# Feed-forward up projection with 512-column matmuls of high and low activations, and halves added on ScalarE and VectorE

## The chip, the cores and the metric

The kernel runs on one NeuronCore of a Trainium2 chip. The metric is the device time of one execution in microseconds, and of several executions the median counts. TensorE (PE) multiplies, VectorE (DVE), ScalarE (ACT) and GpSimd (POOL) do the elementwise work, SyncE (SP) issues most of the loads.

## What is computed

The program is a whole small model: two layers of a first block (feed-forward, mixer, feed-forward; the mixers are a short convolution and a sparse attention) and two layers of a second block. 256 tokens, model width 1024, everything in fp32. The change touches the feed-forward, which the first block calls four times:

```python
def rmsnorm(x, g):
    xf = x.astype(jnp.float32)
    y = xf * lax.rsqrt(jnp.mean(xf * xf, axis=-1, keepdims=True) + EPS)
    return (y * g.astype(jnp.float32)).astype(x.dtype)

def swiglu_ffn(x, w_in, w_out):          # w_in 1024 x 5632, w_out 2816 x 1024
    gate, up = jnp.split(x @ w_in, 2, axis=-1)
    return (jax.nn.silu(gate) * up) @ w_out

for i in range(DEPTH):                   # DEPTH = 2
    if i == N_A_LAYERS:
        kv = shared_kv(h, ...)
    h = h + 0.5 * swiglu_ffn(rmsnorm(h, ffn1_norm[i]), ffn1_w_in[i], ffn1_w_out[i])
    ...                                  # mixer
    h = h + 0.5 * swiglu_ffn(rmsnorm(h, ffn2_norm[i]), ffn2_w_in[i], ffn2_w_out[i])
```

## The kernel before

Activations lie transposed, features on the partitions and the 256 tokens along the row. fp32 products are made of three matmuls of a faster fp32 type (fp32r): a value is split into a high part (rounded to that type) and a low part (the rest), and `mm3` adds high x high, high weight x low activation, and low weight x high activation (lines 712, 713 and 714). The activations are `hnh` and `hnl`, eight tiles of 128 x 256 each; of the weights, `wah`/`wal` hold a chunk of the up projection and `wbh`/`wbl` one of the down projection, two buffers each.

A feed-forward stage walks over 22 chunks of 128 hidden features. `up` of a chunk (PE) makes gate and up, the two sides `g`, over `KT` = 8 k-steps: 2 x 8 x 3 = 48 matmuls into one PSUM bank, 256 columns for each side; banks 4 and 5 take turns. Its end is `gu_ready`. VectorE multiplies the bank by the tokens' factor `rln` into `tmp` (line 1781, `gs_ready`), ScalarE applies silu (line 1332), VectorE multiplies by the up side (1785) and splits the product into `hidh` and `hidl` (1716, 1717, `hid_ready`). `down` of the chunk (PE, `add_rows`) is 8 x 3 = 24 matmuls that add to all 1024 outputs in banks 0 to 3. `staged` sets PE's order: up 0, up 1, down 0, up 2, down 1, and so on to up 21, down 20, down 21. There is no scheduler: each engine runs its own program as it is written, and semaphores tie them together.

Around a chunk, ScalarE also makes the high parts of the weights (`hi_a`, line 1213, and `hi_b`, line 1220), VectorE the low part `wal` (`lo_a`, line 1663) and GpSimd `wbl` (`lo_b`, line 2287); SyncE loads the next raw weights once the low parts have been made. In chunk 0, PE starts each k-step as soon as its activations are there, between two matmuls with zeros that open and close the bank (`open_bank` 717, `close_bank` 720). After it, in stages with `sums`, PE sums the squares (697), ScalarE takes the root and loads the table of silu, and VectorE inverts the root (1653) before line 1781 can run. `open_acc` (725) opens banks 0 to 3. In the first stage VectorE has further `tasks` behind chunks 1, 3, 4, 6 and 7: it copies parameters, reduces angles and makes cosines (lines 1994 to 2013). "Stage" below is one of the four feed-forward stages; in the profile they are at some 16 to 203, 301 to 487, 535 to 727 and 861 to 1046 us.

Of the kernel before, what the change touches and what calls it, by code (L numbers as in the profile page):

```python
# [18 lines left out]
F32R = mybir.dt.float32r  # L19
# [6 lines left out]
P = 128  # L26
# [75 lines left out]
def build(nc, a, out):  # L102
    ctx = ExitStack()
    with ctx:
# [42 lines left out]
        silu, hf = gate_hid[:, 0:2], gate_hid[:, 2:4]  # L147
        hidh, hidl = sb("hidh", [P, 2, T], F32R), sb("hidl", [P, 2, T], F32R)
        hnh, hnl = sb("hnh", [P, KT, T], F32R), sb("hnl", [P, KT, T], F32R)
# [16 lines left out]
        bank = [psum[:, 512 * i:512 * (i + 1)] for i in range(8)]  # L166

# [492 lines left out]
        def _(pe):  # L660
# [85 lines left out]
            def ffn(sums=True, extra=lambda: None, halves=False):  # L746
                n["hn"] += 4

                def up(i, u):
# [4 lines left out]
                    s, at = (n["sa"] + u) % 2, 4 + (n["ffn"] + u) % 2  # L754
                    b = bank[at]
                    if i is FIRST and u == 0:
                        for k in range(KT):
# [3 lines left out]
                            if k == 0:  # L761
                                open_bank(at)
                            for g in range(2):
                                c = slice(g * P, (g + 1) * P)
                                mm3(b[:, g * T:(g + 1) * T], wah[:, s, k, c], wal[:, s, k, c],
                                    hnh[:, k, :], hnl[:, k, :], False, False)
                        close_bank(at).then_inc(S("gu_ready"), 1)
                        return
                    for g in range(2):
                        c = slice(g * P, (g + 1) * P)  # L770
                        for k in range(KT):
                            m = mm3(b[:, g * T:(g + 1) * T], wah[:, s, k, c], wal[:, s, k, c],
                                    hnh[:, k, :], hnl[:, k, :], k == 0, k == KT - 1)
# [7 lines left out]
                def after_first():  # L781
                    if sums:
                        sum_folded()
                    extra()
# [206 lines left out]
            def rest_of_parameters():  # L991
# [3 lines left out]
                pe.wait_ge(S("tcmp_copied"), 1)  # L995
                pe.transpose(bank[6][:, 0:120], vecs[0:120, 0, :], cst[0:120, C_ID:C_ID + 120])
                pe.transpose(bank[6][:, 128:160], vecs[0:32, 1, :], cst[0:32, C_ID:C_ID + 32]
# [13 lines left out]
            for v in range(2):  # L1011
                pe.wait_ge(S("blk_ready"), 8 * (v + 1))
                if v == 1:
                    pe.wait_ge(S("rt_ready"), n["rn"])
                for j in range(16):
                    x = mm(bank[7 - v][:, 0:60], w1s[v][:, j, :], blk[:, v, j, :], start=j == 0, stop=j == 15)
                x.then_inc(S("cmp_ready"), 1)

            ffn(sums=False)

            pe.wait_ge(S("hcmp_ready"), 2)
# [1371 lines left out]
```

## Time and profile before

| | us |
|---|---|
| median of 3 executions | 1385.82 |
| lowest, highest | 1383.04, 1401.29 |
| span of the profiled execution, first to last instruction | 1378.9 |
| PE busy in it | 1301.2 (94%) |
| PE weight loads busy | 1240.3 (90%) |
| DVE, ACT, POOL busy | 869.8, 618.5, 432.9 |

The profiled execution is one of its own; the profile gives its span and no time around it. Its span is 6.9 us below the median. PE stands for the matmuls and PEld for the weight loads that overlap them. Matmuls are pipelined, so a matmul's duration is longer than its pitch, the distance from one start to the next. An idle time in square brackets stands ahead of the instruction, with what ended it.

### The profile page before, as it was taken

What the parts mean: (1) busy time and instruction counts of PE and PEld (TensorE: products, weight loads), DVE (VectorE), ACT (ScalarE), POOL (GpSimd) and SP (SyncE); (2) the same over time, 40 slices, a digit from 0 to 9 for tenths busy, and PEclk for the clock granted to TensorE, in tenths of its full rate; (3) what the DMA queues carried; (4) which work ended last, traced back from release to release, by engine and by line L of the source; (5) the groups of instructions that cost most, each with busy time, mean ns of one, the idle gap of its engine ahead of it and who ended that gap; (6) DMA issues with size and microseconds to landing.
All of it is one profiled execution on the core that took longest, in us unless ns stands there. A gap on an engine that the chain in (4) does not pass through costs nothing.

```text
span 1378.9 us, 27323 instructions
## 1 busy us (share of the span) xinstructions
PE 1301.2 (94%) x10717; PEld 1240.3 (90%) x10717; DVE 869.8 (63%) x1373; ACT 618.5 (45%) x927; POOL 432.9 (31%) x200
## 2 busy tenths in 40 slices
PE   7999999999999998999999889999999998879878
PEld 6999998989999998999999658899999996778768
DVE  6685458786555466444446785755446686875586
ACT  5343344344443355333335685543334436434381
POOL 2444432214444424444440242344441002400041
PEclk8999999999999999999998899999999999999989
DMA  8778655656776546666643215566663453334310
GB/s 257 204 220 242 198 167 152 178 175 203 231 221 183 182 154 176 186 187 189 187 152 126 60 42 152 160 205 185 184 199 97 147 166 147 111 99 146 123 31 32
DMA packets 275115, 222.52 MB, mean 161 GB/s; under 512 B 8098, under 2 KB 256438, under 8 KB 274924
## 3 DMA queue, kind: packets, MB, share of 16 engines
q1 hardware_dynamic: 272528, 215.59, 51.5%
q0 software_dynamic: 1504, 4.49, 1.5%
q10 hardware_dynamic: 1020, 1.58, 0.3%
q8 instruction: 41, 0.67, 0.2%
q14 instruction: 22, 0.18, 0.0%
HBM read 216.40 MB, written 4.19 MB: 160 GB/s over the span
## 4 chain that ended last, share of the span: by engine, by line
PE 76%; DVE 12%; ACT 7%; issue 2%; DMA 1%; ACTq 0%; POOL 0%; DVEq 0%; SPq 0%; POOLq 0%
PE psum L712 24%; PE psum L713 24%; PE psum L714 23%; DVE wal L1663 2%; ACT pbuf L1459 2%; DVE wal L1846 1%; ACT hnh L1294 1%; ACT wah L1213 1%; DVE hnl L1681 1%; DVE hnh L1716 1%; ACT tmp L1459 1%; PE psum L675 1%; ACT arena L1298 1%; ACT wah L1250 1%; PE psum L1141 1%
## 5 line engine op out<-in xcount | busy, mean ns | idle before, releaser
L712 PE MATMUL psum<-hnh,wah 128*128 128x256 f32 (+1 forms) x2176 | 617.6, 284 | 15.0 <-DVE wal L1663 8.2
L713 PE MATMUL psum<-hnl,wah 128*128 128x256 f32 (+1 forms) x2176 | 609.1, 280 | 0.0
L714 PE MATMUL psum<-hnh,wal 128*128 128x256 f32 (+1 forms) x2176 | 608.8, 280 | 0.0
L2287 POOL TENSOR_TENSOR wbl<-raw_b,wbh 128x1024 fp32r<-128x1024 f32 x96 | 324.2, 3378 | 535.2 <-ACT wbh L1220 460.8
L712 PEld LDWEIGHTS psum<-hnh,wah 128*128 128x128 f32 (+1 forms) x2176 | 415.4, 191 | 22.7 <-issue 11.5
L713 PEld LDWEIGHTS psum<-hnl,wah 128*128 128x128 f32 (+1 forms) x2176 | 413.5, 190 | 2.3 <-issue 1.7
L714 PEld LDWEIGHTS psum<-hnh,wal 128*128 128x128 f32 (+1 forms) x2176 | 413.9, 190 | 0.0
L1663 DVE TENSOR_TENSOR wal<-raw_a,wah 128x2048 fp32r<-128x2048 f32 (+1 forms) x128 | 295.5, 2308 | 101.3 <-ACT wah L1213 100.2
L1213 ACT ACTIVATE wah<-raw_a 128x2048 fp32r<-128x2048 f32 (+1 forms) x126 | 237.3, 1884 | 94.0 <-PE psum L714 88.9
L1332 ACT ACTIVATE gate_hid<-tmp 128x256 f32<-128x256 f32 x88 | 36.7, 417 | 430.4 <-DVE tmp L1781 430.4
L712 PE MATMUL psum<-hidh,wbh 128*128 128x256 f32 x768 | 213.2, 278 | 0.9 <-DVE hidl L1717 0.9
L713 PE MATMUL psum<-hidl,wbh 128*128 128x256 f32 x768 | 213.0, 277 | 0.0
L714 PE MATMUL psum<-hidh,wbl 128*128 128x256 f32 x768 | 213.0, 277 | 0.0
L1781 DVE TENSOR_TENSOR tmp<-psum,rms 128x512 f32<-128x512 f32 x88 | 60.8, 691 | 224.1 <-PE psum L714 217.0
L712 PEld LDWEIGHTS psum<-hidh,wbh 128*128 128x128 f32 x768 | 145.0, 189 | 1.1 <-DVE hidl L1717 1.1
L714 PEld LDWEIGHTS psum<-hidh,wbl 128*128 128x128 f32 x768 | 144.2, 188 | 0.0
L713 PEld LDWEIGHTS psum<-hidl,wbh 128*128 128x128 f32 x768 | 144.1, 188 | 0.0
L2350 POOL TENSOR_SCALAR pbuf<-pbuf,rs 128x256 f32<-128x256 f32 x36 | 33.9, 951 | 334.9 <-DVE rs L1903 258.5
L1220 ACT ACTIVATE wbh<-raw_b 128x1024 fp32r<-128x1024 f32 x96 | 100.2, 1044 | 8.5 <-PE psum L714 4.3
L1785 DVE TENSOR_TENSOR gate_hid<-gate_hid,tmp 128x256 f32<-128x256 f32 x88 | 39.5, 449 | 43.3 <-ACT gate_hid L1332 43.3
L1459 ACT ACTIVATE pbuf<-pbuf,nmx 128x256 f32<-128x256 f32 (+1 forms) x108 | 44.0, 410 | 6.5 <-DVE nmx L1896 3.8
L1294 ACT ACTIVATE hnh<-hres,par 128x256 fp32r<-128x256 f32 x72 | 31.4, 499 | 30.4 <-DVE hres L1736 19.2
(298 smaller groups left out, 1510.3 us busy)
## 6 DMA issues: line engine op xcount, KB each, us to landing
raw_a<-in_ffn_w_in SPq DMA_DIRECT2D x176, 512.0 KB, 5.1
raw_b<-in_ffn_w_out SPq DMA_DIRECT2D x88, 512.0 KB, 5.0
raw_a<-in_w_in_even SPq DMA_DIRECT2D x15, 1024.0 KB, 5.3
raw_a<-in_conv_w_in SPq DMA_DIRECT2D x24, 512.0 KB, 4.1
raw_a<-in_w_in_odd SPq DMA_DIRECT2D x11, 1024.0 KB, 5.3
raw_a<-in_w_kv SPq DMA_DIRECT2D x6, 1024.0 KB, 5.5
raw_b<-in_conv_w_out SPq DMA_DIRECT2D x8, 512.0 KB, 5.7
raw_a<-in_attn_w_q SPq DMA_DIRECT2D x4, 1024.0 KB, 5.2
```

Source lines behind the costliest of these rows:

```text
L712: mm(dst, wh, xh, start=start, stop=False)
L713: mm(dst, wh, xl, start=False, stop=False)
L714: return mm(dst, wl, xh, start=False, stop=stop)
L1213: act.activation(wah[:, s, :, 0:w], raw_a[:, wa.slot(u), :, 0:w], ACT.Copy).then_inc(S("a_hi"), 1)
L1220: act.activation(wbh[:, s], raw_b[:, s], ACT.Copy).then_inc(S("b_hi"), 1)
L1294: x = act.activation(hnh[:, t, :], hres[:, t, :], ACT.Copy, scale=gains[:, g, t:t + 1])
L1332: act.activation(silu[:, gs, :], tmp[:, gs, 0:T], ACT.Silu).then_inc(S("silu_ready"), 1)
L1459: x = act.activation(p[:, lo:hi], p[:, lo:hi], ACT.Exp, scale=-1.0 if duos[st]["kind"] == "full" else 1.0, bias=nmx[:, r, i:i + 1], accum_ ...
L1663: v.tensor_tensor(wal[:, s, :, 0:w], raw_a[:, (n["ra"] + u) % 2, :, 0:w], wah[:, s, :, 0:w].bitcast(F32), ALU.subtract).then_inc(S("a_lo"), 1)
L1781: v.tensor_tensor(tmp[:, gs, :].rearrange("p (g c) -> p g c", g=2), bank[4 + gs][:, :].rearrange("p (g c) -> p g c", g=2), rln[:, None, :] ...
L1785: link(v.tensor_tensor(hf[:, hs, :], silu[:, gs, :], tmp[:, gs, T:2 * T], ALU.mult))
L2287: g.tensor_tensor(wbl[:, s], raw_b[:, s], wbh[:, s].bitcast(F32), ALU.subtract).then_inc(S("b_lo"), 1)
```

## The change

PE's two matmuls with the same high weights become one of 512 columns: high activations on the left, low ones on the right, into one whole bank per side. For that the activations are one tensor `hn2`. The matmul of the low weights and the high activations stays, 256 columns, on the left half. A chunk now takes two banks, 4 and 5 for even chunks and 6 and 5 for odd ones, so bank 5 is used by each chunk for the second side, and `up` waits in its middle for the addition of the chunk before. ScalarE copies both right halves into `halves_sb` (`low_copied`), VectorE adds them to the left halves into `tmp` (`gs_ready`) and then multiplies `tmp` by `rln` in place (`gu_scaled`), and silu comes after that. The zero matmuls of chunk 0 go. As bank 6 is now taken, the transposed parameters and the compression's products move to other banks, with the waits that go with them.

```diff
-        hnh, hnl = sb("hnh", [P, KT, T], F32R), sb("hnl", [P, KT, T], F32R)
+        hn2 = sb("hn2", [P, 2, KT, T], F32R)
+        hnh, hnl = hn2[:, 0], hn2[:, 1]
...
+        halves_sb = ptb[:, :, :].rearrange("p a c -> p (a c)")[:, 0:1024].rearrange("p (b g c) -> p b g c", b=2, g=2)
+
+        def up_banks(p):
+
+            return bank[4 + 2 * p], bank[5]
+
+        def up_halves(p, half):
+
+            both = psum[:, 512 * (4 + p):512 * (6 + p)].rearrange("p (b c) -> p b c", b=2)
+            return both[:, :, half * T:(half + 1) * T]
...
                     pe.wait_ge(S("gs_ready"), n["ffn"] + u + 1 + 2 * i)
-                    s, at = (n["sa"] + u) % 2, 4 + (n["ffn"] + u) % 2
-                    b = bank[at]
+                    s, pair = (n["sa"] + u) % 2, up_banks((n["ffn"] + u) % 2)
+
+                    def product(g, k):
+
+                        c = slice(g * P, (g + 1) * P)
+                        mm(pair[g][:, :], wah[:, s, k, c], hn2[:, :, k, :], start=k == 0, stop=False)
+                        return mm(pair[g][:, 0:T], wal[:, s, k, c], hnh[:, k, :], start=False, stop=k == KT - 1)
+
                     if i is FIRST and u == 0:
                         for k in range(KT):
                             if halves and k % 4 == 0:
                                 pe.wait_ge(S("first_lo"), k // 4 + 1)
                             wait_hn(k)
-                            if k == 0:
-                                open_bank(at)
                             for g in range(2):
-                                c = slice(g * P, (g + 1) * P)
-                                mm3(b[:, g * T:(g + 1) * T], wah[:, s, k, c], wal[:, s, k, c],
-                                    hnh[:, k, :], hnl[:, k, :], False, False)
-                        close_bank(at).then_inc(S("gu_ready"), 1)
+                                m = product(g, k)
+                        m.then_inc(S("gu_ready"), 1)
                         return
                     for g in range(2):
-                        c = slice(g * P, (g + 1) * P)
+                        if g == 1:
+                            pe.wait_ge(S("gs_ready"), n["ffn"] + u + 2 + 2 * i)
                         for k in range(KT):
-                            m = mm3(b[:, g * T:(g + 1) * T], wah[:, s, k, c], wal[:, s, k, c],
-                                    hnh[:, k, :], hnl[:, k, :], k == 0, k == KT - 1)
+                            m = product(g, k)
                     m.then_inc(S("gu_ready"), 1)
...
-                    act.wait_ge(S("gs_ready"), n["ffn"] + u + 3 + 2 * i)
-                    act.activation(silu[:, gs, :], tmp[:, gs, 0:T], ACT.Silu).then_inc(S("silu_ready"), 1)
+                    act.wait_ge(S("gu_ready"), n["ffn"] + u + 1 + 2 * i)
+                    act.activation(halves_sb[:, gs], up_halves(gs, 1), ACT.Copy).then_inc(S("low_copied"), 1)
+                    act.wait_ge(S("gu_scaled"), n["ffn"] + u + 1 + 2 * i)
+                    act.activation(silu[:, gs, :], raw_gate[gs], ACT.Silu).then_inc(S("silu_ready"), 1)
...
-                    v.wait_ge(S("gu_ready"), n["ffn"] + u + 1 + 2 * i)
-                    v.tensor_tensor(tmp[:, gs, :].rearrange("p (g c) -> p g c", g=2),
-                                    bank[4 + gs][:, :].rearrange("p (g c) -> p g c", g=2),
-                                    rln[:, None, :].to_broadcast([P, 2, T]), ALU.mult).then_inc(S("gs_ready"), 1)
+                    gu = tmp[:, gs, :].rearrange("p (g c) -> p g c", g=2)
+                    v.wait_ge(S("low_copied"), n["ffn"] + u + 1 + 2 * i)
+                    v.tensor_tensor(gu, up_halves(gs, 0), halves_sb[:, gs], ALU.add).then_inc(S("gs_ready"), 1)
+                    v.wait_ge(S("gs_ready"), n["ffn"] + u + 3 + 2 * i)
+                    v.tensor_tensor(gu, gu, rln[:, None, :].to_broadcast([P, 2, T]), ALU.mult
+                                    ).then_inc(S("gu_scaled"), 1)
                     v.wait_ge(S("silu_ready"), n["ffn"] + u + 1 + 2 * i)
-                    link(v.tensor_tensor(hf[:, hs, :], silu[:, gs, :], tmp[:, gs, T:2 * T], ALU.mult))
+                    link(v.tensor_tensor(hf[:, hs, :], silu[:, gs, :], raw_up[gs], ALU.mult))
```

PE in the loop of the first stage, from the last steps of an `up` into `down`, before:

```order
L714 MATMUL psum<-hnh,wal 128x256
L712 MATMUL psum<-hnh,wah 128x256
L713 MATMUL psum<-hnl,wah 128x256
L714 MATMUL psum<-hnh,wal 128x256
L777 REGISTER_ALU
L712 MATMUL psum<-hidh,wbh 128x256
L713 MATMUL psum<-hidl,wbh 128x256
```

and now, where the first side of an `up` ends and the second begins:

```order
L772 MATMUL psum<-hn2,wah 128x512
L773 MATMUL psum<-hn2,wal 128x256
L772 MATMUL psum<-hn2,wah 128x512
L773 MATMUL psum<-hn2,wal 128x256
L786 REGISTER_ALU
L772 MATMUL psum<-hn2,wah 128x512
L773 MATMUL psum<-hn2,wal 128x256
L772 MATMUL psum<-hn2,wah 128x512
```

Three matmuls a step have become two, and a register instruction for the new wait stands in the middle of the chunk, between the sides.

VectorE in the same loop, one chunk from `gu_ready` to `lo_a`, before:

```order
L1780 REGISTER_ALU
L1781 TENSOR_TENSOR tmp<-psum,rms 128x512
L1785 TENSOR_TENSOR gate_hid<-gate_hid,tmp 128x256
L285 REGISTER_ALU
L1716 CAST hidh<-gate_hid 128x256
L285 REGISTER_ALU
L1717 TENSOR_TENSOR hidl<-gate_hid,hidh 128x256
L1661 REGISTER_ALU
L1663 TENSOR_TENSOR wal<-raw_a,wah 128x2048
```

and now:

```order
L1796 REGISTER_ALU
L1797 TENSOR_TENSOR tmp<-psum,ptb 128x512
L1798 REGISTER_ALU
L1799 TENSOR_TENSOR tmp<-tmp,rms 128x512
L1802 TENSOR_TENSOR gate_hid<-gate_hid,tmp 128x256
L298 REGISTER_ALU
L1731 CAST hidh<-gate_hid 128x256
L298 REGISTER_ALU
L1732 TENSOR_TENSOR hidl<-gate_hid,hidh 128x256
L1678 TENSOR_TENSOR wal<-raw_a,wah 128x2048
```

The multiplication from PSUM has become an addition from PSUM and `ptb` (where `halves_sb` lies) and a multiplication of `tmp`; the rest keeps its order.

## Rows read from the trace of the kernel before

**Rows 1.** Busy time in 20 us windows: PE busy (instructions), PEclk, DMA share, GB/s.

```profile
140.00:160.00 20.00, 20.00 (x179) 1.00 0.82 234
...
640.00:660.00 20.00, 20.00 (x172) 1.00 0.58 182
```

**Rows 2.** Timeline of PE, first FFN: start, duration, line, operands.

```profile
139.91 0.28 PE L712 MATMUL psum<-hnh,wah 128*128 128x256 f32 x1
...
140.93 0.28 PE L712 MATMUL psum<-hidh,wbh 128*128 128x256 f32 x1
```

**Rows 3.** Timeline of PE, third FFN.

```profile
640.03 0.28 PE L712 MATMUL psum<-hidh,wbh 128*128 128x256 f32 x1
...
640.74 0.28 PE L712 MATMUL psum<-hnh,wah 128*128 128x256 f32 x1
```

**Rows 4.** Timeline of PE, end of chunk 0 of the third FFN.

```profile
545.92 0.39 PE L720 MATMUL psum<-zero 128*128 128x512 bf16 x1
546.14 1.03 PE L725 MATMUL psum<-zero 128*128 128x512 bf16 x4
547.36 0.38 PE L712 MATMUL psum<-hnh,wah 128*128 128x256 f32 x1 [0.19 <-issue]
```

**Rows 5.** Timeline of PE: 48-column matmuls, ten apart.

```profile
742.23 0.39 PE L713 MATMUL psum<-wal,hnh 128*128 128x48 f32 x1
...
744.37 0.39 PE L714 MATMUL psum<-wah,hnl 128*128 128x48 f32 x1
```

**Rows 6.** Window of those: PE, PEld, DVE, ACT, POOL busy (instructions), PEclk, DMA.

```profile
742.00:745.00 3.00, 3.00 (x15) 3.00 (x16) 0.63 (x1) 1.21 (x1) 0.00 (x0) 0.50 1.08 382
```

**Rows 7.** Groups by line and form: busy us, mean ns, idle before.

```profile
L1283 ACT ACTIVATE arena<-psum 128x512 f32<-128x512 f32 x8 | 4.8, 597 | 15.5 <-PE psum L714 14.9 <-PE psum L741 0.4
...
L1785 DVE TENSOR_TENSOR gate_hid<-gate_hid,tmp 128x256 f32<-128x256 f32 x88 | 39.5, 449 | 43.3 <-ACT gate_hid L1332 43.3
```

**Rows 8.** Timelines of ScalarE, VectorE and GpSimd, mid third FFN.

```profile
647.32 0.42 ACT L1332 ACTIVATE gate_hid<-tmp 128x256 f32<-128x256 f32 x1 [5.31 <-DVE tmp L1781]
...
649.58 2.29 DVE L1663 TENSOR_TENSOR wal<-raw_a,wah 128x2048 fp32r<-128x2048 f32 x1 [0.51 <-ACT wah L1213]
...
650.57 3.55 POOL L2287 TENSOR_TENSOR wbl<-raw_b,wbh 128x1024 fp32r<-128x1024 f32 x1 [4.93 <-ACT wbh L1220]
```

**Rows 9.** Timelines of VectorE and GpSimd, chunks 3 to 6 of the first FFN.

```profile
51.37 0.69 DVE L1781 TENSOR_TENSOR tmp<-psum,rms 128x512 f32<-128x512 f32 x1 [2.88 <-PE psum L714]
...
54.35 2.29 DVE L1663 TENSOR_TENSOR wal<-raw_a,wah 128x2048 fp32r<-128x2048 f32 x1 [0.60 <-ACT wah L1213]
56.79 2.26 DVE L1999 CAST arena<-arena 128x256 f32<-128x256 int32 x1
...
61.95 0.69 DVE L1781 TENSOR_TENSOR tmp<-psum,rms 128x512 f32<-128x512 f32 x1
...
79.19 1.22 DVE L1785 TENSOR_TENSOR gate_hid<-gate_hid,tmp 128x256 f32<-128x256 f32 x1 [0.48 <-ACT gate_hid L1332]
...
83.55 2.40 DVE L2012 TENSOR_TENSOR rope<-rope 128x256 f32<-128x256 f32 x1
...
76.58 3.56 POOL L2287 TENSOR_TENSOR wbl<-raw_b,wbh 128x1024 fp32r<-128x1024 f32 x1 [6.59 <-ACT wbh L1220]
```

**Rows 10.** Timelines of VectorE and PE, last chunk of the first FFN.

```profile
200.21 0.43 DVE L1717 TENSOR_TENSOR hidl<-gate_hid,hidh 128x256 fp32r<-128x256 f32 x1
...
200.77 0.31 PE L712 MATMUL psum<-hidh,wbh 128*128 128x256 f32 x1
```

**Rows 11.** Timelines of ScalarE, VectorE and PE, head of the second FFN.

```profile
313.99 0.20 ACT L1348 ACTIVATE lut<-eps 128x1 f32<-128x1 f32 x1
...
314.77 0.69 DVE L1781 TENSOR_TENSOR tmp<-psum,rms 128x512 f32<-128x512 f32 x1 [0.31 <-DVE rms L1653]
...
317.23 4.49 DVE L1663 TENSOR_TENSOR wal<-raw_a,wah 128x2048 fp32r<-128x2048 f32 x1
...
321.78 0.38 PE L712 MATMUL psum<-hnh,wah 128*128 128x256 f32 x1 [1.08 <-DVE wal L1663]
```

More of the change, by code:

```diff
@@ L147, in build @@
         silu, hf = gate_hid[:, 0:2], gate_hid[:, 2:4]
+        raw_gate, raw_up = (tmp[:, 0, 0:T], tmp[:, 1, T:2 * T]), (tmp[:, 0, T:2 * T], tmp[:, 1, 0:T])
         hidh, hidl = sb("hidh", [P, 2, T], F32R), sb("hidl", [P, 2, T], F32R)
-        hnh, hnl = sb("hnh", [P, KT, T], F32R), sb("hnl", [P, KT, T], F32R)
+        hn2 = sb("hn2", [P, 2, KT, T], F32R)
+        hnh, hnl = hn2[:, 0], hn2[:, 1]
         zero = sb("zero", [P, 512], BF16)
@@ L783, in after_first @@
                         sum_folded()
+                    if halves:
+                        pe.wait_ge(S("tcmp_copied"), 1)
                     extra()
@@ L994, in rest_of_parameters @@
                 pe.wait_ge(S("norms_loaded"), 16 * (6 - NGAIN))
-                pe.wait_ge(S("tcmp_copied"), 1)
-                pe.transpose(bank[6][:, 0:120], vecs[0:120, 0, :], cst[0:120, C_ID:C_ID + 120])
-                pe.transpose(bank[6][:, 128:160], vecs[0:32, 1, :], cst[0:32, C_ID:C_ID + 32]
+                pe.wait_ge(S("rt_ready"), n["rn"])
+                pe.transpose(bank[7][:, 0:120], vecs[0:120, 0, :], cst[0:120, C_ID:C_ID + 120])
+                pe.transpose(bank[7][:, 128:160], vecs[0:32, 1, :], cst[0:32, C_ID:C_ID + 32]
                              ).then_inc(S("par_turned"), 1)
@@ L1012, in _ @@
                 pe.wait_ge(S("blk_ready"), 8 * (v + 1))
-                if v == 1:
-                    pe.wait_ge(S("rt_ready"), n["rn"])
                 for j in range(16):
-                    x = mm(bank[7 - v][:, 0:60], w1s[v][:, j, :], blk[:, v, j, :], start=j == 0, stop=j == 15)
+                    x = mm(bank[v][:, 0:60], w1s[v][:, j, :], blk[:, v, j, :], start=j == 0, stop=j == 15)
                 x.then_inc(S("cmp_ready"), 1)
-            ffn(sums=False)
-            pe.wait_ge(S("hcmp_ready"), 2)
+            ffn(sums=False, extra=lambda: pe.wait_ge(S("hcmp_ready"), 2))
             def q_between(c):
@@ L1524, in _ @@
                 act.wait_ge(S("cmp_ready"), v + 1)
-                act.activation(hcmp[:, v, :], bank[7 - v][:, 0:60], ACT.Gelu_apprx_tanh).then_inc(S("hcmp_ready"), 1)
+                act.activation(hcmp[:, v, :], bank[v][:, 0:60], ACT.Gelu_apprx_tanh).then_inc(S("hcmp_ready"), 1)
             ffn("q", sums=False)
@@ L1993, in copy_parameters @@
                 v.wait_ge(S("par_turned"), 2)
-                v.tensor_copy(par[:, 16:120], bank[6][:, 16:120])
-                link(v.tensor_copy(par[:, 128:160], bank[6][:, 128:160]))
+                v.tensor_copy(par[:, 16:120], bank[7][:, 16:120])
+                link(v.tensor_copy(par[:, 128:160], bank[7][:, 128:160]))
                 v.sem_inc(S("par_ready"), 1)
```

## The prediction

> **What bounds the kernel now.** I read the windows first, then PE's timeline at two places, then ScalarE, VectorE and GpSimd around one chunk, and last the head and the tail of a feed-forward stage. In the windows TensorE is busy for the whole 20 us at full granted clock in mid-stage [rows 1], so inside the four FFN stages a nanosecond off TensorE's pitch is a nanosecond off the time, as long as nobody else falls behind. The same rows show two paces: 179 matmul records in 20 us in the first FFN, 172 in the third. The timeline gives the pitch: nine matmuls in 1.02 us, 113.3 ns each [rows 2], and six in 0.71 us, 118 ns [rows 3]. Streaming 256 columns at 2.4 GHz takes 106.7 ns, so 6.6 or 11 ns per matmul is something else. Windows of the whole run have 178 or 179 records through stages one, two and four and 172 or 173 through stage three; I count three fast stages and one slow one.
>
> What the rest may be: the matmuls of only 48 columns stand ten apart in 2.14 us, 214 ns each [rows 5], at half clock [rows 6], where 48 columns stream in 40 ns. So what sets their pitch is not columns; it is 256 cycles, most simply the load of 128 columns of fp32 weights. A weight load as long as a 256-column matmul sits beside each of the kernel's matmuls, a tie, and 6.6 ns is what the tie costs.
>
> **Part 1, TensorE.** A k-step and side of the up projection has three 256-column matmuls and three weight loads; now it has one of 512, one of 256, and two loads. Columns stay 768. Before: 3 x 113.3 = 340 ns (fast), 3 x 118 = 353 ns (slow, by 117.8). After: the 512-column matmul has twice the time that its neighbour's load needs. The nearest rows are the bf16 zero matmuls of 512 columns: the one at 545.92 is followed at 546.14, and four of them take 1.03 us with the last one's 0.39 in it, so (1.03 - 0.39)/3 = 0.213, 0.22 by the first pair [rows 4]; I take 217 ns. The 256-column one keeps its tie, 113 ns. Sum 330 ns: 10 ns less in a fast stage, and in the slow one 18 to 23, of which I take 18, since the 256-column matmul may keep the slow pace. A stage has 22 chunks x 16 steps = 352. Three fast stages: 3 x 3.5 = 10.5 us; the slow one 6.4 us. Where the head of a stage waits for others anyway (below) some 0.8 us of this is lost. **Gain 16.1 us.** Bounds: at 213 + 109 ns (half of 217 for 256 columns) the steps gain 17.5 and 31 ns, and the down projections of stage three 528 x 4.5 ns = 2.4, 31 us in all; with a 512-column pitch of 2 x 113.3 the gain is nil.
>
> The Trainium skill ("TensorE: Matmul & The Clock Gate", "Back-to-back issue gap") gives a gap of N/2.4 + 2.5 ns for isolated matmuls and says that real streams are set by load and matmul together. By the formula a step would go from 3 x 109.2 to 215.8 + 109.2 ns and the whole change would win 3.5 us. The pitch of [rows 2], 113.3, is above the formula, so here the trace disagrees with it and I stay with the row.
>
> The opening and closing zero matmuls of chunk 0 go too, 0.43 us per stage. In the first, second and fourth stages another wait (parameters, weights' low part) ends behind them, so they give nothing; in the third they count.
>
> **Part 2, the longer way from `gu_ready` to `hid_ready`.** Before: one VectorE multiplication from PSUM, then silu. Now: ScalarE copies 512 columns out of two banks (nearest row 597 ns from one bank [rows 7]), VectorE adds (nearest row 0.69 us, the old multiplication, PSUM and SBUF in [rows 9]), and the multiplication follows with SBUF operands at about the same 0.69. With 0.03 us per hand-over the way grows by 0.60 + 0.69 + 0.07 = 1.36 us.
> Mid-stage this lies under other work: ScalarE sat idle 5.31 us before silu [rows 8], VectorE 2.88 us before the multiplication [rows 9], and `down` of a chunk comes only after another `down` and the next `up`, 2.7 + 5.4 us after its `gu_ready`. ScalarE's `hi_a` and `hi_b`, queued behind its new wait for `gu_scaled`, come 1.4 us later, and so do VectorE's `lo_a`, GpSimd's `lo_b` and the loads that wait for them; each has at least that in hand.
> At a stage's **tail** it does not: the last `down` needs the last chunk after one other `down` only, and the split that ends at 200.64 is followed by the matmul at 200.77 [rows 10], with no slack. All of 1.36 us shows: 4 x 1.36 = 5.4 us.
> At the **head** of stages two and four: ScalarE's table load and its small activation end at 314.19, and only then can the copy run, so the addition starts near 314.85 and the multiplication near 315.6 in place of 314.77. Behind it stand silu, the split, and the `lo_a` that takes 4.49 us and for which TensorE waits (1.08 us before 321.78) [rows 11]. So 0.9 us each, 1.8 us. The third stage has no root, but TensorE waits there for the evacuation of chunk 0 (it resumes at 547.36 [rows 4]): +0.63 for copy and addition against -0.43 for the zero matmuls, +0.2.
>
> **Part 3, the new wait inside `up`.** The second side of each chunk writes bank 5, which both parities share, and waits for the previous chunk's addition. The matmuls behind it, and with them everything, stand. It is due 2.7 (`down`) + 2.7 (first side) = 5.4 us after `gu_ready`, and mid-stage the addition ends at 1.4. But in the first FFN, VectorE has two angle reductions of 5.2 us (from 56.79 to 61.95; the second is the same instructions) and two cosine steps with a 2.40 us instruction [rows 9]. A chunk's own VectorE work there is 54.35 + 2.29 - 51.37 = 5.27 us [rows 9], now + 0.72 + 0.15 between chunks = 6.14. Stepping through with 8.0 us per chunk: the chunk before the first reduction ends at 58.0, the reduction at 63.35, the next addition at 64.05 (due 64.7); that chunk at 69.35, the second reduction at 74.7, the addition at 75.4, due 72.7: 2.7 us of standing. The cosines, in the same way, give 0.5 and 0.9. Sum 4.1 us.
>
> **Sum:** -16.1 + 5.4 + 1.8 + 0.2 + 4.1 = -4.6 us. The profiled execution's span is 1378.9 us, 6.9 below the median of 1385.8; I let the change of the span stand for that of the median: **1381 us**.
>
> **Rivals.**
> (a) The pitch is proportional to columns: 113.3 ns is 256 columns at some rate, and the 512-column one takes 227. For it: no row shows an fp32r matmul of another width that columns bind. Against it: [rows 4 to 6]. No gain, all costs: 1385.8 + 11.5 = 1397. The change loses from a 512-column pitch of some 0.225 on.
> (b) The page's formula, gain 3.5 us, costs 11.5: 1394.
> (c) Loads matter more than I take, 322 ns a step: 1385.8 - 31 + 0.8 + 11.5 = 1367.
> (d) **VectorE and GpSimd become the bound.** The new multiplication reads SBUF twice. Such VectorE instructions are held while GpSimd runs: the product at 79.19 took 1.22 us [rows 9] in place of a mean of 0.449 [rows 7], beside GpSimd's from 76.58 to 80.14 [rows 9]. GpSimd in turn seems to work only from the end of `lo_a` on, for some 2.3 us: 650.57 + 3.55 is 2.25 behind 649.58 + 2.29 [rows 8]. If the multiplication waits for that in each chunk, the loop is 2.3 + 5.3 = 7.6 us against TensorE's 8.0 (16 x 0.330 + 24 x 0.1133), close, but still hidden. If each `lo_a` took the 4.49 us of [rows 11] it is 6.14 + 2.2 = 8.34, and 84 chunks x 0.34 = 29 us on top: 1410. From 8.4 per chunk the kernel is slower by over 2%. Against it: GpSimd's work is released one `hi_b` after `hi_a`, so `lo_a` goes first in mid-stage.
> The Trainium skill ("SBUF — State Buffer", "SBUF: two separate sides") calls this pair of ports an exclusive lock, held for the whole instruction by whoever starts first. The trace agrees with the 1.22 us above; it changes nothing in the sum.
> (e) An fp32r matmul of 512 columns runs in two passes, 0.45 us: 1408 x 0.21 = +296, near 1690. Nothing here shows it.
>
> **Chances.** My sum, 1374 to 1389: 0.50. (a) 0.14, (b) 0.08, (c) 0.10, (d) 0.12, a third of it past 2%, (e) 0.02; 0.04 for a mix of paces in between. A measurement tells some 2% (28 us) of this kernel from no change. Faster by over 2% needs more than the widest gain: 0.02. Slower: 0.04 + 0.02 + 0.01 = 0.07. Within: 0.91. The range takes in (c), (a) and the lower half of (d): 1366 to 1400.
>
> **What would show it.** Right: pitch of 0.217 behind a 512-column matmul and 0.113 behind a 256-column one, also in the third stage; a chunk of 8.0 us; at each tail an idle of 1.4 us of TensorE for the split; one idle of some 2.7 us on the addition near 73 us. Wrong if the first pitch is 0.227 (a), if 256-column ones fall to 0.109 (c), if TensorE idles for `lo_a` or the addition in every chunk (d), or if the slow pace, which I can't predict, moves to other stages: 4.5 ns x 1,584 is 7 us per stage.

## The result: 1411.6 us, 1.8% slower, outside the predicted range

The changed kernel takes 1411.58 us, median of 4 runs (1406.09 to 1412.54); the kernel before 1384.43 us, median of 4 (1374.80 to 1401.29). The ratio is 1.0183, 95% interval 1.0141 to 1.0225. It and the ratios below leave out slow executions, those over 1.5% above the fastest of the same kernel, among them one of e1_split (1407.2 us) and one of e10_cut_once (1406.7 us). The forecast was 1381 us within 1366 to 1400. The profiled execution took 1411.98 us with a span of 1410.2 us, 31.3 us more than the span before.

From the page of the changed kernel, first the busy time of each engine, then four groups (line, engine, operation, operands, count; busy us, mean ns; idle before them):

```profile
PE 1322.1 (94%) x9287; PEld 1194.3 (85%) x9301; DVE 935.7 (66%) x1461; ACT 670.1 (48%) x1015; POOL 433.9 (31%) x200
...
L772 PE MATMUL psum<-hn,wah 128*128 128x512 f32 x1408 | 507.1, 401 | 13.3 <-DVE wal L1678 8.0
L773 PE MATMUL psum<-hn,wal 128*128 128x256 f32 x1408 | 397.4, 282 | 0.0
...
L1797 DVE TENSOR_TENSOR tmp<-psum,ptb 128x512 f32<-128x512 f32 x88 | 60.9, 692 | 182.5 <-ACT ptb L1345 180.2
L1345 ACT ACTIVATE ptb<-psum 128x512 f32<-128x512 f32 x88 | 52.5, 597 | 242.6 <-PE psum L773 242.5
```

By the program, 1408 matmuls and as many weight loads of the up projection are gone, and TensorE stays the bound. The new copy takes the 597 ns and the new addition the 692 ns that were forecast. The time went to TensorE's pitch. Its timeline in the first FFN, where [rows 2] had 113.3 ns per matmul:

```profile
142.14 0.28 PE L773 MATMUL psum<-hn,wal 128*128 128x256 f32 x1
142.25 0.40 PE L772 MATMUL psum<-hn,wah 128*128 128x512 f32 x1
142.49 0.28 PE L773 MATMUL psum<-hn,wal 128*128 128x256 f32 x1
...
143.55 0.28 PE L773 MATMUL psum<-hn,wal 128*128 128x256 f32 x1
```

Four k-steps from 142.14 to 143.55: 353 ns each, 0.235 us behind a 512-column matmul and 0.118 behind a 256-column one. That is exactly what three 256-column matmuls took in the slow third FFN of before [rows 3], and 13 ns more than in the fast stages. The down projections, which the change does not touch, are slow too. Third FFN:

```profile
641.26 0.28 PE L725 MATMUL psum<-hidh,wbh 128*128 128x256 f32 x1
...
642.44 0.28 PE L726 MATMUL psum<-hidl,wbh 128*128 128x256 f32 x1
```

Ten matmuls in 1.18 us, 118 ns each. It is so in all four FFN stages: a chunk takes 16 x 0.3534 + 24 x 0.1178 = 8.48 us, where before it took 8.16 in three stages and 8.48 in the third. The granted clock is no part of it. The windows (PE busy and matmul records, granted clock, DMA share, GB/s), which answer to [rows 1]:

```profile
140.00:160.00 20.00, 20.00 (x137) 1.00 0.79 229
640.00:660.00 20.00, 20.00 (x140) 1.00 0.69 205
```

TensorE is busy throughout at full granted clock. Three stages x 22 chunks x 0.32 us = 21 us of the 31.3. Of the rest, 2.8 us lie behind the last feed-forward stage (332.0 us from the last `down` to the end before, 334.7 now), where the change adds no work; in the runs below this stretch takes from 331 to 336 us. What is left is mainly waits: the profile's list for PE (what it waited for: us in total, times, longest), then one place of each kind.

```profile
PE psum L772 <- DVE wal L1678: 8.0, 6, 3.6
...
PE psum L725 <- DVE hidl L1732: 4.9, 5, 1.0
...
PE psum L772 <- DVE tmp L1797: 2.9, 4, 1.5
```

```profile
76.78 0.51 PE L772 MATMUL psum<-hn,wah 128*128 128x512 f32 x1 [1.49 <-DVE tmp L1797]
...
210.91 0.39 PE L725 MATMUL psum<-hidh,wbh 128*128 128x256 f32 x1 [1.01 <-DVE hidl L1732]
...
322.10 0.50 PE L772 MATMUL psum<-hn,wah 128*128 128x512 f32 x1 [0.72 <-DVE wal L1678]
...
332.37 0.50 PE L772 MATMUL psum<-hn,wah 128*128 128x512 f32 x1 [1.00 <-DVE wal L1678]
```

The first is the wait inside `up` on the previous chunk's addition, beside the angle reductions of the first FFN. The second is a stage's tail, where [rows 10] had no slack. The other two are the head of the second FFN [rows 11].

Mid-stage the longer way is hidden, as forecast. ScalarE and VectorE around one chunk:

```profile
147.75 0.60 ACT L1345 ACTIVATE ptb<-psum 128x512 f32<-128x512 f32 x1 [3.23 <-PE psum L773]
...
148.38 0.69 DVE L1797 TENSOR_TENSOR tmp<-psum,ptb 128x512 f32<-128x512 f32 x1 [2.48 <-ACT ptb L1345]
149.11 0.69 DVE L1799 TENSOR_TENSOR tmp<-tmp,rms 128x512 f32<-128x512 f32 x1
```

Both engines still stand idle before their first instruction of a chunk, 3.23 and 2.48 us. Beside GpSimd the new multiplication is sometimes held, in 7 of its 88 cases (1.3 to 1.94 us in place of 0.69), five of them in the first FFN. The longest, with GpSimd at work from 80.73 to 84.29:

```profile
82.90 1.94 DVE L1799 TENSOR_TENSOR tmp<-tmp,rms 128x512 f32<-128x512 f32 x1
```

The same sum of columns costs the same at half clock too. In chunk 0 of the third FFN the granted clock is 0.50 (third line, a window), and there a 512-column matmul is followed after 0.43 us and a 256-column one after 0.21:

```profile
557.20 0.63 PE L772 MATMUL psum<-hn,wah 128*128 128x512 f32 x1
557.63 0.41 PE L773 MATMUL psum<-hn,wal 128*128 128x256 f32 x1
...
557.20:560.40 3.20, 3.20 (x11) 0.50 0.85 248
```

That is 0.64 us a step, as much as three 256-column matmuls of 0.213 us at that clock.

### The profile page after: what moved, and what is told of

Read it like the earlier page. It is cut to its first block, busy times and chain, and to the rows that moved or that the text cites. A ratio compares the mean times of both kernels' runs of the same rounds, so it can differ in the third digit from the quotient of the medians.

```text
span 1410.2 us, 24706 instructions
## 1 busy us (share of the span) xinstructions
PE 1322.1 (94%) x9287; PEld 1194.3 (85%) x9301; DVE 935.7 (66%) x1461; ACT 670.1 (48%) x1015; POOL 433.9 (31%) x200
## 4 chain that ended last, share of the span: by engine, by line
PE 73%; DVE 14%; ACT 8%; issue 3%; DMA 1%; POOL 0%; DVEq 0%; ACTq 0%; POOLq 0%
PE psum L772 22%; PE psum L725 12%; PE psum L726 12%; PE psum L727 12%; PE psum L773 11%; DVE wal L1678 3%; ACT pbuf L1474 2%; ACT wah L1226 1%; DVE hn L1696 1%; ACT hn L1307 1%; DVE wal L1863 1%; ACT tmp L1474 1%; DVE rstd L1660 1%; DVE hn L1731 1%; DVE tmp L1797 1%
## 5 line engine op out<-in xcount | busy, mean ns | idle before, releaser
L772 PE MATMUL psum<-hn,wah 128*128 128x512 f32 x1408 | 507.1, 401 | 13.3 <-DVE wal L1678 8.0
L773 PE MATMUL psum<-hn,wal 128*128 128x256 f32 x1408 | 397.4, 282 | 0.0
L772 PEld LDWEIGHTS psum<-hn,wah 128*128 128x128 f32 x1408 | 267.0, 190 | 78.9 <-DVE wal L1678 7.3
L773 PEld LDWEIGHTS psum<-hn,wal 128*128 128x128 f32 x1408 | 266.5, 189 | 0.0
L725 PE MATMUL psum<-hn,wah 128*128 128x256 f32 x768 | 223.3, 291 | 21.2 <-DVE hn L1696 9.1
L725 PE MATMUL psum<-hidh,wbh 128*128 128x256 f32 x768 | 216.1, 281 | 5.0 <-DVE hidl L1732 4.9
L726 PE MATMUL psum<-hn,wah 128*128 128x256 f32 x768 | 216.6, 282 | 0.0
L727 PE MATMUL psum<-hn,wal 128*128 128x256 f32 x768 | 216.4, 282 | 0.0
L1797 DVE TENSOR_TENSOR tmp<-psum,ptb 128x512 f32<-128x512 f32 x88 | 60.9, 692 | 182.5 <-ACT ptb L1345 180.2
L1345 ACT ACTIVATE ptb<-psum 128x512 f32<-128x512 f32 x88 | 52.5, 597 | 242.6 <-PE psum L773 242.5
L725 PEld LDWEIGHTS psum<-hn,wah 128*128 128x128 f32 x768 | 147.3, 192 | 17.9 <-issue 9.2
L726 PEld LDWEIGHTS psum<-hn,wah 128*128 128x128 f32 x768 | 146.9, 191 | 1.9 <-issue 1.7
L727 PEld LDWEIGHTS psum<-hn,wal 128*128 128x128 f32 x768 | 147.0, 191 | 0.0
```

Of the source, the lines that this page charges most:

```text
L725: mm(dst, wh, xh, start=start, stop=False)
L726: mm(dst, wh, xl, start=False, stop=False)
L727: return mm(dst, wl, xh, start=False, stop=stop)
L772: mm(pair[g][:, :], wah[:, s, k, c], hn2[:, :, k, :], start=k == 0, stop=False)
L773: return mm(pair[g][:, 0:T], wal[:, s, k, c], hnh[:, k, :], start=False, stop=k == KT - 1)
L1345: act.activation(halves_sb[:, gs], up_halves(gs, 1), ACT.Copy).then_inc(S("low_copied"), 1)
```

## The experiments

Two questions. Is the slow pace the work of the 512-column matmul, or of something else in the change (the new waits, the two pieces of the moving operand) or of chance? And what do the copies and waits cost when the pace is left out of the comparison? Eleven kernels ran. Below, **fast** is a pitch of 113.3 ns per 256 columns and **slow** one of 117.8; both were read from the starts of the matmuls in each trace.

| run | us (median, runs) | kernel before beside it | ratio (95%) |
|---|---|---|---|
| e1_split | 1392.76 (10) | 1386.34 | 1.0030 (0.9982 to 1.0077) |
| e2_contig | 1409.90 (4) | 1386.34 | 1.0131 (1.0068 to 1.0194) |
| e3_chunk0 | 1392.62 (10) | 1386.34 | 1.0018 (0.9980 to 1.0055) |
| e4_side0 | 1410.30 (4) | 1386.34 | 1.0142 (1.0080 to 1.0204) |
| e5_set_reset | 1407.29 (1) | 1384.96 | single run |
| e6_one_wide | 1397.75 (10) | 1384.96 | 1.0090 (1.0058 to 1.0123) |
| e7_two_narrow | 1393.55 (10) | 1384.96 | 1.0046 (1.0006 to 1.0086) |
| e8_cut_loop | 1380.13 (12) | 1383.21 | 0.9972 (0.9947 to 0.9996) |
| e9_split_cut | 1390.88 (12) | 1383.21 | 1.0051 (1.0021 to 1.0080) |
| e10_cut_once | 1377.68 (12) | 1383.21 | 0.9951 (0.9924 to 0.9978) |
| e11_grouped | 1391.53 (1) | 1383.21 | single run |

### The wide matmul split, all else as changed

```diff
-mm(pair[g][:, :], wah[:, s, k, c], hn2[:, :, k, :], start=k == 0, stop=False)
+mm(pair[g][:, T:2 * T], wah[:, s, k, c], hnl[:, k, :], start=k == 0, stop=False)
+mm(pair[g][:, 0:T], wah[:, s, k, c], hnh[:, k, :], start=False, stop=False)
```

> The changed kernel, with each 512-column matmul of the up projection written as two of 256 columns into the same two halves of the same bank; copies, addition, waits and banks stay as changed. Theory 1 (a 512-column fp32r matmul streams at the slow pace, 0.46 ns a column, and leaves the matmuls behind it there): the stages go back to 113.3 ns per matmul, 340 ns a step, 8.16 us a chunk; what is left over the kernel before are only the longer tails, heads and the waits on the addition, some 10 us, so about 1394 us. Theory 2 (the slow pace is set by what happens at the stage's start or at the new waits inside the up projection, not by the width): the pace stays at 117.8 in all four stages, 353 ns a step, and the time stays at 1410 or above.

Measured 1392.8 us. Windows in the four FFN stages:

```profile
160.00:180.00 20.00, 20.00 (x178) 1.00 0.62 187
400.00:420.00 20.00, 20.00 (x172) 1.00 0.80 232
640.00:660.00 20.00, 20.00 (x179) 1.00 0.74 219
940.00:960.00 20.00, 20.00 (x179) 1.00 0.71 216
```

The fast pace is back in three stages (178 or 179 records, as in [rows 1]); the second is slow, and so is the first up to 74 us, where TensorE stands for a wait. So with the copies, the addition and the wait in place, the width alone takes some 19 us. But which stage is slow has moved: in the kernel before it was the third. Nine of the ten runs spread from 1381.5 to 1401.8, those of the changed kernel only from 1406.1 to 1412.5. It looks as if with 256-column matmuls a stage gets one of the two paces by chance, and with 512-column ones always the slow one. No kernel was profiled twice, so the chance is inferred, from the spread and from which stage is slow in which kernel.

### The moving operand in one piece

```diff
-hn2 = sb("hn2", [P, 2, KT, T], F32R)
+hn2 = sb("hn2", [P, KT, 2, T], F32R)
...
-mm(pair[g][:, :], wah[:, s, k, c], hn2[:, :, k, :], start=k == 0, stop=False)
+mm(pair[g][:, :], wah[:, s, k, c], hn2[:, k, :, :].rearrange("p a c -> p (a c)"), start=k == 0, stop=False)
...
```

> The changed kernel, with the high and low activations laid out side by side for each 128 rows, so that the 512 moving columns of a matmul are one contiguous piece instead of two pieces of 256 that lie 8 KB apart. Theory 3 (the two pieces slow the read of the moving operand): the 512-column pitch falls from 235 ns to 217 to 227 and the 256-column ones return to 113, 330 to 340 ns a step; 22 x 4 x 16 steps x 13 to 23 ns is 18 to 32 us less than the changed kernel, 1380 to 1393 us. Theories 1 and 2: 235 and 118 ns stay, and the time stays within 3 us of 1411.

Measured 1409.9 us, and 235 and 118 ns throughout. Theory 3 falls: the two pieces of the operand play no part.

### Wide matmuls in chunk 0 only

```diff
+if i is FIRST and u == 0:
     mm(pair[g][:, :], wah[:, s, k, c], hn2[:, :, k, :], start=k == 0, stop=False)
+else:
+    mm(pair[g][:, T:2 * T], wah[:, s, k, c], hnl[:, k, :], start=k == 0, stop=False)
+    mm(pair[g][:, 0:T], wah[:, s, k, c], hnh[:, k, :], start=False, stop=False)
```

> The changed kernel with 512-column matmuls only in the first chunk of each feed-forward stage; in the other 21 chunks of a stage each is two of 256 columns into the same places. Theory 1 with a pace that sticks until TensorE next stands idle: all of a stage stays at 117.8 ns, some 1408 us. Theory 1 without sticking (the width acts only on its neighbours): chunk 0 alone is slow, then 113.3 ns, some 1395 us, within 2 us of the run in which all are split. Theory 2: as the run in which all are split, whatever that gives.

Measured 1392.6 us, as with all of them split. In chunk 0 a wide matmul is followed after 235 ns, but behind it TensorE waits (for the low part of the weights, for the root), and behind a restart the pace can be another: in this profile the second stage is slow and the other three fast. So the slow pace need not outlive a stop of TensorE. My expectation for a sticking pace, 1408, had overlooked that chunk 0 is followed by waits.

This profile also shows what the wait inside `up` can cost where the first stage is fast. The granted clock of the window is 0.50:

```profile
76.19 0.58 PE L775 MATMUL psum<-hn,wah 128*128 128x256 f32 x1 [2.68 <-DVE tmp L1801]
...
76.60:79.30 2.70, 2.70 (x14) 0.50 0.57 150
```

The idle time is the 2.7 us that I had forecast. Behind it 13 matmuls are 0.213 us apart, 0.1 us each above the pace of this stage: 1.3 us that the forecast did not have.

### Wide matmuls on one side only

```diff
+if g == 0:
     mm(pair[g][:, :], wah[:, s, k, c], hn2[:, :, k, :], start=k == 0, stop=False)
+else:
+    mm(pair[g][:, T:2 * T], wah[:, s, k, c], hnl[:, k, :], start=k == 0, stop=False)
+    mm(pair[g][:, 0:T], wah[:, s, k, c], hnh[:, k, :], start=False, stop=False)
```

> The changed kernel with 512-column matmuls only on the first of the two sides of each chunk; on the second side each is two of 256 columns. Theory 1 without sticking: the second side and the down projections run at 113.3 ns, only the 512-column matmuls themselves and their neighbours at the slow pace, so half of the loss: 88 chunks x 8 steps x 13.4 ns is 9.4 us above the run in which all are split, about 1404 us. Theory 1 with sticking: slow throughout, 8.48 us a chunk, about 1410 us. Theory 2: as the run in which all are split.

Measured 1410.3 us, slow but for short stretches behind waits (41 matmuls at most), the 48 matmuls of 256 columns between one group of wide ones and the next included: 5.07 us from 142.81 to 147.88 for 43 of them, 118 ns. So half of the wide matmuls cost as much as all of them. The pace sticks through a stream that nothing interrupts, and theory 2 falls with this and the first run.

### One wide matmul in two chunks, and three things to undo it

On the kernel with all split. In odd chunks, at side 0, k = 4, the 512-column matmul; in even chunks at the same place, one thing for each stage:

```diff
+here = i is not FIRST and g == 0 and k == 4
+if here and u == 1:
+    mm(pair[g][:, :], wah[:, s, k, c], hn2[:, :, k, :], start=False, stop=False)
...
+if here and stage_no[0] == 1:
+    for q in range(2):
+        mm(pair[g][:, T + P * q:T + P * q + P], wah[:, s, k, c], hnl[:, k, P * q:P * q + P], start=False, stop=False)
...
+if here and stage_no[0] == 2:
+    mm(pair[g][:, :], zero[:, 0:P], zero[:, :], start=False, stop=False)
+if here and stage_no[0] == 3:
+    mm(pair[g][:, 0:P], zero[:, 0:P], zero[:, 0:P], start=False, stop=False)
```

> The kernel with all wide matmuls split, but with one 512-column matmul (side 0, k = 4) in every second chunk of each stage, the odd ones. In the even chunks at the same step stands something else: in stage one the 256-column matmul on the low part is two of 128 columns, in stage two a bf16 zero matmul of 512 columns is added, in stage three a bf16 zero matmul of 128 columns, in stage four nothing. If one 512-column matmul sets the slow pace and the pace sticks until the stream is broken, the matmuls before the first 512-column one have whatever pace the stage began with and all behind it have 117.8 ns, in stage four to its end. If the pace acts only on neighbours, stage four stands at 113.3 ns but for one or two matmuls in each second chunk. If one of the three insertions sets the fast pace, its stage shows 113.3 ns from each insertion to the next 512-column matmul, ten times over; if none does, stages one to three look like stage four.

Measured 1407.3 us, one run. TensorE's timeline in stage one, at the wide matmul and then at the cut, 8.5 us later:

```profile
150.45 0.28 PE L789 MATMUL psum<-hn,wal 128*128 128x256 f32 x1
150.56 0.39 PE L777 MATMUL psum<-hn,wah 128*128 128x512 f32 x1
150.79 0.28 PE L789 MATMUL psum<-hn,wal 128*128 128x256 f32 x1
...
151.50 0.28 PE L789 MATMUL psum<-hn,wal 128*128 128x256 f32 x1
...
159.03 0.33 PE L781 MATMUL psum<-hn,wah 128*128 128x128 f32 x2
159.20 0.34 PE L788 MATMUL psum<-hn,wah 128*128 128x256 f32 x1
...
160.08 0.28 PE L789 MATMUL psum<-hn,wal 128*128 128x256 f32 x1
...
160.64 0.28 PE L788 MATMUL psum<-hn,wah 128*128 128x256 f32 x1
```

From 150.79 on 118 ns (six in 0.71 us), from 160.08 on 113 (five in 0.56 us). It went like this at every cut of stage one and at every insertion of stage three: fast behind each, slow behind each wide matmul. Eight of the ten cuts and all ten insertions met a slow stream. In stage four, with nothing inserted, the stream came back fast from a wait behind the first wide matmul, and from the second wide matmul (908.17) on all stayed slow, nine groups of 142 matmuls between one wide matmul and the next. Stage two went the other way round: behind the zero matmul of 512 columns slow, ten times, and behind the fp32r one at 231 ns fast, ten times. So a wide matmul does not simply set the slow pace: it can also lift a stream out of it. What decides that, the runs don't show. The matmul of 128 columns did set the fast pace each time.

The price of a single wide matmul goes with what it does. Here and in the next run together, 43 met a fast stream: 225 or 226 ns (twice 113.3 is 226.7), slow behind each. Of the 45 that met a slow one, 32 took 230 to 233 ns and left it fast, and 13 took 235 or 236 (twice 117.8) and left it slow.

### The kernel before, with one more matmul of 512 columns in two chunks, or two of 256

```diff
+if g == 0 and k == 4 and u == 1:
+    pe.wait_ge(S("rt_ready"), n["rn"])
+    if not sums:
+        pe.wait_ge(S("hcmp_ready"), 2)
+    mm(bank[7][:, :], wah[:, s, k, c], hnh[:, 4:6, :], start=True, stop=True)
```

The other kernel has the same waits, and in place of the last line two matmuls of 256 columns, on `hnh[:, 4, :]` and `hnh[:, 5, :]`, into the two halves of the bank.

> The kernel before, with one 512-column fp32r matmul added in every second chunk of the up projection, 40 or 44 in all, into an unused bank. Its own time is 44 x 0.235 = 10 us at most. If a 512-column matmul sets a slow pace that sticks, the three stages that were fast go slow as well, 22 x 0.32 = 7 us each: 1378.9 + 10 + 21 = 1410 us, and no run far below 1408. If not: 1389 us, spread as before by some 25 us over the runs.

> The same addition to the kernel before as in the run with one wide matmul, but as two matmuls of 256 columns. Both theories: own time 44 x 0.23 = 10 us, no effect on the pace, so 1386 + 10 = 1396 us, and runs spread over some 20 us as the kernel before's are. Only if the added work itself (its waits, the unused bank) slows the stream does it come out at 1410 too.

Measured 1397.75 us with the wide one (1394.3 to 1399.2), 1393.55 with the two narrow ones (1384.9 to 1404.1). I had expected 1410 for the first: wrong; 1396 for the second held. The windows show why (between one added matmul and the next, twice in a row):

```profile
149.00:163.00 14.00, 14.00 (x126) 1.00 0.73 207
166.00:180.00 14.00, 14.00 (x121) 1.00 0.63 185
```

The pace changes at 42 of the 44 added wide matmuls, from slow to fast at 148.54 and back at 165.09, in all four stages, so about half of the matmuls are slow. That gives 1371.9 (span with all four stages fast: 1378.9 less the third stage's 7.0) + 2 x 7.0 + 44 x 0.2285 = 1396.0, and the span was 1396.0, to the tenth by luck. In the run with two narrow ones all four stages were fast in mid-stage (the second only from 325 us on), its span was 1384.6, and it spreads like the kernel before. The kernel before ran from 1376.2 to 1395.3 us in its 19 runs here; four stages at 7.0 us each would be enough for that, and the next runs test it.

### A cut that sets the fast pace, in both kernels

In the kernel before, the low-part matmul of one step in an even chunk as two of 128 columns; the same in the changed kernel with its wide matmuls split (the first run). Both then differ by the copies, the addition, the waits and the zero matmuls of chunk 0, at one pace.

```diff
+if g == 0 and k == 4 and u == 2:
+    mm(b[:, 0:T], wah[:, s, k, c], hnh[:, k, :], start=False, stop=False)
+    for q in range(2):
+        mm(b[:, q * P:(q + 1) * P], wah[:, s, k, c], hnl[:, k, q * P:(q + 1) * P], start=False, stop=False)
+    m = mm(b[:, 0:T], wal[:, s, k, c], hnh[:, k, :], start=False, stop=False)
+    continue
```

> The kernel before, in which one 256-column matmul (side 0, k = 4) of every even chunk from the second on is written as two of 128 columns, 40 in all; the arithmetic is the same. Theory (in the earlier run this cut was followed by the 113.3 ns pace each time, whatever stood before): all four feed-forward stages at 113.3 ns. Price of a cut, from that run: 57 + 113 + 170 ns for what else takes 227, some 0.12 us, 5 us in all. The kernel before has one slow stage in its profile (span 1378.9) and by its median near 1385 some two of four: 1371.9 + 5 = 1377 us of span, 1379 us of time, and the runs closer together than before's. If the cut does not decide the pace: 1385 + 5 = 1390, with before's spread.

> The changed kernel with all its wide matmuls split in two, and with the cut in every even chunk. It has the copies, the addition, the longer way to the down projection and the wait inside the up projection of the changed kernel, and the matmuls of the kernel before, all at one pace. Against the run with the same cuts in the kernel before it gives the price of these parts alone: predicted 5.4 + 1.8 + 0.2 + 4.1 = 11.5 us; from the two traces some 10 us, so near 1389 us. If the waits cost nothing and the pace was all: 1379.

Measured 1380.1 us (1376.3 to 1382.3 in 12 runs, where before had 1375.1 to 1393.9 in 29), and 1390.9 us (1385.8 to 1395.8). With the pace set in the four stages, two thirds of the kernel before's spread are gone. In both profiles the stream is fast in all four stages behind every one of the cuts; nearly all of the cuts met it fast already, so that these two runs show that it stays so and little on how a cut sets it. The difference is 10.8 us; by the two ratios 0.8% of 1383, with some 5 us of uncertainty. The two profiled spans, 1380.5 and 1390.1, differ by 9.6. Where it is, by PE's waits, first in the kernel before with cuts, then in the changed one with split and cuts:

```profile
PE psum L712 <- DVE hidl L1723: 0.9, 1, 0.9
```

```profile
PE psum L725 <- DVE hidl L1737: 5.6, 6, 1.1
...
PE psum L776 <- DVE tmp L1802: 4.4, 4, 2.1
```

The list has idle time alone. By the starts of the matmuls, the `down` before the last and the last one, first with cuts:

```profile
199.91 0.28 PE L712 MATMUL psum<-hidh,wbh 128*128 128x256 f32 x1
...
202.63 0.30 PE L712 MATMUL psum<-hidh,wbh 128*128 128x256 f32 x1
```

and with split and cuts:

```profile
202.50 0.28 PE L725 MATMUL psum<-hidh,wbh 128*128 128x256 f32 x1
...
206.50 0.38 PE L725 MATMUL psum<-hidh,wbh 128*128 128x256 f32 x1 [1.12 <-DVE hidl L1737]
```

It is 2.72 and 4.00 us in all four stages, so the tails cost 4 x 1.28 = 5.1 us more, and the wait inside `up` 4.4. With these the 9.6 us of the spans are used up. The waits for the weights' low part, which would show dearer heads, come to 11.8 us in the one and 11.9 in the other.

### The cut once per stage

The same cut in chunk 2 alone; TensorE's first two trips of the loop's body are written out so that it can stand there alone.

> As the run with a cut in every even chunk, but TensorE's first two trips through the loop body stand apart, and only chunk 2 of each stage has the cut: 4 in all. If the pace set there sticks to the end of the stage: four fast stages for 0.5 us, span near 1372, time near 1374, ratio to before about 0.992. If it drifts back in the 19 chunks behind: as before, 1385.

```profile
160.00:180.00 20.00, 20.00 (x178) 1.00 0.53 157
400.00:420.00 20.00, 20.00 (x179) 1.00 0.76 222
640.00:660.00 20.00, 20.00 (x179) 1.00 0.63 188
940.00:960.00 20.00, 20.00 (x179) 1.00 0.58 176
```

Four fast stages from four cuts: the pace holds for the remaining 19 chunks and 1425 matmuls in a row. Two of the four met a slow stream, and it was fast behind them. 1377.7 us, 0.5% under the kernel before (interval 0.2 to 0.8%): small, but with the cut in every even chunk (0.3%, interval 0.0 to 0.5%) it is one of the two versions here that beat the kernel before. It came out 3.7 us above my 1374. The stretches outside the FFN stages still have both paces: some 1,480 of their 256-column matmuls are slow in this profile, and some 1,255 in that of before, whose third stage adds 1,535. The 225 more are 1 us of the 3.7.

### All wide matmuls of a side first, then all narrow ones

```diff
-for k in range(KT):
-    m = product(g, k)
+c = slice(g * P, (g + 1) * P)
+for k in range(KT):
+    mm(pair[g][:, :], wah[:, s, k, c], hn2[:, :, k, :], start=k == 0, stop=False)
+for k in range(KT):
+    m = mm(pair[g][:, 0:T], wal[:, s, k, c], hnh[:, k, :], start=False, stop=k == KT - 1)
```

> The changed kernel, in each side of a chunk first the eight 512-column matmuls one after another, then the eight of 256 columns. If a wide matmul streams at the slow rate in itself: 235 ns apart and 118 behind, 8.48 us a chunk, 1411 us. If it is only the alternation of wide and narrow that keeps the slow pace: the wide ones 227 apart, 340 ns a step, some 1390 us. If the load hidden behind a wide matmul is worth what the prediction took: 217 apart, 1383 us.

TensorE's timeline over one side (eight wide, eight narrow, then the down projection):

```profile
141.53 1.32 PE L789 MATMUL psum<-hn,wah 128*128 128x512 f32 x5
...
143.39 1.07 PE L791 MATMUL psum<-hn,wal 128*128 128x256 f32 x8
144.30 0.28 PE L725 MATMUL psum<-hidh,wbh 128*128 128x256 f32 x1
```

Eight wide ones in 1.86 us, 232 ns each, then eight narrow ones in 0.91 us, 114 each: none of my three cases. In the starts the first wide one takes 226 ns and the others 236 and 231 in turn, and the narrow stream behind them is fast again in mid-stage. So a stream of wide matmuls was not cheaper than the same columns in narrow ones at the fast pace (2 x 113.3 = 227). Only the order differs from the changed kernel, so it is the alternation of wide and narrow that keeps that one in the slow pace; this rests on one run. Its 1391.5 us is about what the changed kernel costs without that.

## Why the prediction was wrong, point by point

**Part 1, the pitch of a wide matmul, is the step that failed.** It was taken at 217 ns from the bf16 zero matmuls [rows 4], on the reasoning that 6.6 ns of each 113.3 was a tie with a weight load [rows 5, 6] that a wide matmul would escape. An fp32r matmul of 512 columns took 235 or 236 ns in 1,360 of 1,408 cases, and never under 225. Taking a load away gave nothing: 512 + 256 columns cost 353 ns, what 3 x 256 cost at the slow pace; at half clock it was 0.64 us against 3 x 0.213. So the term "10 ns less in a fast stage, 18 in the slow one", the 16.1 us of gain, was nothing, and with it the tie that a wide matmul was to escape. The bf16 row was the wrong neighbour, although it had the right width. The chance of 0.14 on "the pitch is proportional to columns" (rival a) was too low: no row showed an fp32r matmul that columns bound, and I let a row of another type decide. The single wide matmuls that met a fast stream took 225 or 226 ns, rival (a)'s 227. Its remark that the change loses from a pitch of 0.225 on was wrong by the forecast's own sum: a gain of 4.6 us over 1408 matmuls is gone with 3.3 ns, at 0.220.

**The slow pace is what no case of mine held.** Rival (a) ended at 1397 because it kept the fast pace in three stages. I had counted the paces by stage in the windows, and named at the end that the slow one might move (7 us per stage), but gave that no chance of its own and no room in the range. The changed kernel has it in all four: with the split run 19 us less, with alternation broken (grouped) 20 us less, with contiguous operands nothing. The gain of 16.1 us became a loss of 21 against the profiled execution: 37 us.

**Part 2 and Part 3 held but for the heads.** 5.4 + 1.8 + 0.2 + 4.1 = 11.5 us were forecast, 10.8 measured at one pace by the medians and 9.6 by the spans: tails 5.1 for 5.4, wait inside `up` 4.4 for 4.1, and for the heads at most what is left, where I had 2.0. In the changed kernel itself the waits on the addition are shorter (2.9 us, longest 1.49 in place of 2.7). The likely reason is that at 8.48 us per chunk the addition is due later: in the chunk-0 run, with a fast first stage, it was 2.68.

**The sum** with what was measured: 1378.9 + 3 x 7.0 + 10.8 = 1410.7 us, or 1409.5 with 9.6; the span was 1410.2. That it is so close is in part luck, since 2.8 us of the span's growth lie behind the last of these stages and the waits on the addition are 1.5 us shorter than in the run that gave the 10.8.

**Rivals.** (b), 215.8 ns for a wide matmul, and (c), loads that matter more, fall with the 235 ns. (d): VectorE and GpSimd are not the bound; the multiplication is held at 82.90 and in six other places, and this costs TensorE at most its share of the 2.9 us. (e), two passes, falls: 235, not 450. Its price was also off: 1408 x (0.45 - 0.227) is 314 us, not 296.

**The reference point.** Before's median stood 6.9 us above its profiled span. That was more than the 1.8 us by which the later profiled executions' times exceed their spans. The profiled execution had one slow stage; the median run may have had nearer two, which no profile shows. I carried the 6.9 over as if it were constant.

## What to carry to other kernels

Before a wider matmul is costed, ask for a row of the same data type: here bf16 with 512 columns took 217 ns and fp32r with as many 235. When windows of equal work show two rates at full clock and no waits, treat the rate as a state of its own: find out whether a stage has it by chance, ask what the change does to it, and put it into the range, since here it was worth more than the instructions saved. And a change that saves a third of the weight loads of a stretch, as here, can gain nothing where loads already run beside the matmuls.

## What the hardware showed that I had not expected

An unbroken stream of fp32r matmuls of 256 columns runs at one of two pitches, 113.3 or 117.8 ns, both at full granted clock, and keeps it: 1,425 in a row at the first (each stage with the cut once), 1,535 at the second (third stage of the kernel before). Which one it is seems to be drawn when the stream restarts, after a wait or after matmuls of another kind; stage three was slow in one profile, stage two in two others, none in a fourth. A matmul of 128 columns in the stream, of fp32r or of bf16 zeros, left it fast every time, also the 21 times that it met a slow one, at some 0.12 us for the cut. A single one of 512 columns left a fast stream slow every time, and a slow one sometimes fast (32 times, most of them in the kernel before with one wide matmul added) and sometimes slow (13 times, most of them in stage four of the run with one in two chunks). Its price was that of two 256-column ones: 226 ns from the fast pace, 235 or 236 within the slow one, 231 where it led from slow to fast. Why the length matters at all, and what the two paces are inside the engine, stays open.
